# SSD stage of a two-block model: another order of ScalarE's work and of C B, y's gate on VectorE and its square on GpSimd

## The reference, cut to what matters

```python
zxbcdt = h @ w_in
xbc = silu(causal_depthwise_conv(xbc, conv_w, conv_b))      # -> xs, b_in, c_in
a_cs = cumsum(a_dt)
decay = exp(where(causal, a_cs[..., :, None] - a_cs[..., None, :], -inf))
cb = einsum('bclgn,bcsgn->bcgls', c_c, b_c)
y = einsum('bcgjls,bcsgjp->bclgjp', cb * decay, xdt)          # (+ the part of earlier chunks)
y = y + xs * repeat(d_skip, HEAD_DIM)
g = y * silu(z)
g = g * rsqrt(mean(g * g) + EPS)                             # the mean over a group's 256 channels
out = (g * norm_g) @ w_out
```

## Time and profile before

| what | value |
|---|---|
| median of 3 runs | 1209.87 us (1209.8 to 1210.95) |
| the profiled execution's own time | 1210.28 us |
| its span, first to last instruction | 1208.6 us |
| mean granted TensorE clock | 0.973 |
| the stretch from the end of slot 1 to the end of slot 7 on ScalarE | 73.4 to 223.8 us |

### The profile page before, as it was taken

How to read it: one execution, slowest core, us unless ns; L and a number is a source line. 1 busy time by engine, 2 the same in 40 slices (tenths; PEclk the granted TensorE clock), 3 DMA queues, 4 the chain that set the end, 5 groups by cost and what they waited for, 6 DMA issues and landing times.

```text
span 1208.6 us, 23743 instructions
## 1 busy us (share of the span) xinstructions
PE 1148.3 (95%) x8898; PEld 1089.9 (90%) x8898; DVE 754.4 (62%) x1123; ACT 674.9 (56%) x1071; POOL 186.3 (15%) x134
## 2 busy tenths in 40 slices
PE   6999999999999999679988999999999999999998
PEld 5988988899999999556657999999998999999998
DVE  4788778768665554536646666555678678666543
ACT  4788888755554343457735555444554665555332
POOL 0443444317000001022301000000000212000000
PEclk8999999999999999779979999999999999999999
DMA  5554344395555554222203555565544555555553
GB/s 192 179 173 151 130 158 154 113 256 159 180 174 168 182 165 157 88 86 88 80 26 111 186 191 181 183 192 179 170 159 125 172 185 184 188 177 188 192 179 99
DMA packets 53225, 190.32 MB, mean 157 GB/s; under 512 B 5920, under 2 KB 7072, under 8 KB 53168
## 3 DMA queue, kind: packets, MB, share of 16 engines
q1 hardware_dynamic: 51408, 182.95, 47.0%
q0 software_dynamic: 1760, 6.59, 1.8%
HBM read 188.44 MB, written 1.08 MB: 157 GB/s over the span
## 4 chain that ended last, share of the span: by engine, by line
PE 75%; DVE 8%; issue 8%; ACT 5%; POOL 3%; DMA 1%; ACTq 0%; DVEq 0%; POOLq 0%; SPq 0%
PE lin L412 23%; PE lin L414 22%; PE lin L413 22%; DVE w_lo L1207 2%; POOL w_lo L1747 1%; ACT w_hi L826 1%; POOL y L1765 1%; PE lin L641 1%; PE ps L682 1%; PE ps L683 1%; PE lin L639 1%; DVE cv L1286 1%; PE ps L445 1%; DVE rot_a L1509 0%; DVE x_lo L1217 0%
## 5 line engine op out<-in xcount | busy, mean ns | idle before, releaser
L1207 DVE TENSOR_TENSOR w_lo<-w_raw,w_hi 128x1024 fp32r<-128x1024 f32 x303 | 381.3, 1260 | 273.1 <-ACT w_hi L826 273.0
L826 ACT ACTIVATE w_hi<-w_raw 128x1024 fp32r<-128x1024 f32 (+2 forms) x343 | 354.3, 1040 | 244.3 <-PE lin L414 239.9
L412 PE MATMUL lin<-x_hi,w_hi 128*128 128x256 f32 (+1 forms) x1528 | 445.4, 291 | 11.0 <-DVE x_lo L1233 3.7
L414 PE MATMUL lin<-x_hi,w_lo 128*128 128x256 f32 (+1 forms) x1528 | 439.0, 287 | 0.0
L413 PE MATMUL lin<-x_lo,w_hi 128*128 128x256 f32 (+1 forms) x1528 | 438.2, 287 | 0.0
L412 PEld LDWEIGHTS lin<-x_hi,w_hi 128*128 128x128 f32 x1528 | 292.0, 191 | 15.2 <-DVE x_lo L1233 4.1
L413 PEld LDWEIGHTS lin<-x_lo,w_hi 128*128 128x128 f32 x1528 | 291.5, 191 | 1.4 <-issue 1.0
L414 PEld LDWEIGHTS lin<-x_hi,w_lo 128*128 128x128 f32 x1528 | 292.3, 191 | 0.0
L414 PE MATMUL lin<-hid_hi,w_lo 128*128 128x256 f32 (+1 forms) x768 | 218.2, 284 | 0.0
L413 PE MATMUL lin<-hid_lo,w_hi 128*128 128x256 f32 (+1 forms) x768 | 217.9, 284 | 0.0
L412 PE MATMUL lin<-hid_hi,w_hi 128*128 128x256 f32 (+1 forms) x768 | 217.4, 283 | 0.0
(11 more groups left out here) (252 smaller groups left out, 1515.7 us busy)
## 6 DMA issues: line engine op xcount, KB each, us to landing
w_raw<-w SPq DMA_DIRECT2D x343, 512.0 KB, 3.3
acs_bc<-acs_dram POOLq DMA_DIRECT2D x8, 544.0 KB, 4.9
bias_mask<-rpb POOLq DMA_DIRECT2D x4, 512.0 KB, 9.6
h<-h SPq DMA_DIRECT2D x4, 272.0 KB, 3.7
out<-h SPq DMA_DIRECT2D x8, 128.0 KB, 3.4
cst<-const SPq DMA_DIRECT2D x1, 784.0 KB, 8.4
vecs<-vec SPq DMA_DIRECT2D x1, 131.5 KB, 2.1
acs_dram<-y POOLq DMA_DIRECT2D x1, 34.0 KB, 2.5
```

The source lines that it names most:

```text
L412: mm3(o, wh, xh, start=first and i == 0, stop=False)
L414: ins = mm3(o, wl, xh, start=False, stop=last and i == kts - 1)
L826: a(w_hi[pg.slot][:, 0:n], w_raw[pg.slot][:, 0:n], ACT.Copy).then_inc(w_hi_done, pages)
L1207: tt(w_lo[pg.slot][:, 0:n], w_raw[pg.slot][:, 0:n], w_hi[pg.slot][:, 0:n].bitcast(F32), ALU.subtract)\
```

## The change

ScalarE's slot has another order: the decays first, then z's sigmoid, then `hi` and `conv0` of the first pair, `decay_logs(s, 0)` before the first sigmoid of the slot (for s above 0), and `decay_logs(s, 1)` and the second sigmoid ahead of `g_hi`. TensorE does C B before the transposes. VectorE masks C B before the convolution, takes the product y2 = y1 * z_s, and does the first SiLU product before `lo` of page (c+3, 0). GpSimd squares y2, which ScalarE did before.

```diff
 TensorE
                 if has_scan:
+                    cb_products(s + (-1))
                     x_transposes(s + (-1))
-                    cb_products(s + (-1))
 ScalarE
-                if has_lin:
-                    hi((c + 2).page(0))
-                    hi((c + 2).page(1))
                 if has_scan:
                     decay(g, 0)
                     decay(g, 1)
-                if has_stat:
-                    act.wait_ge(y2_done, (gs + 1).value)
-                    a(h_sq[:, 0:2, :], y2[:, :, :], ACT.Square).then_inc(ysq_done, 1)
-                if has_lin:
-                    conv0(s, 0)
-                    hi((c + 3).page(0))
-                    act.wait_ge(clamped, s.times(2, 1).value)
-                    sigmoid(sg[:, 0:2, :], sg_step, s.times(6))
-                if has_scan:
                     kz = g.times(3, K_GRP + 2)
                     act.wait_ge(drained[kz.parity], kz.half + 1)
                     sigmoid(z_sg[:, :, :], zg_step, g.times(3), z_raw[:, :, :])
                 if has_lin:
+                    hi((c + 2).page(0))
+                    conv0(s, 0)
+                    hi((c + 2).page(1))
+                if has_lin:
+                    if s.base:
+                        decay_logs(s, 0)
+                    act.wait_ge(clamped, s.times(2, 1).value)
+                    sigmoid(sg[:, 0:2, :], sg_step, s.times(6))
+                    hi((c + 3).page(0))
                     conv0(s, 1)
                     hi((c + 3).page(1))
                 if not has_lin:
                     hi2(s + (C_SOUT - 6))
-                if has_lin and s.base:
-                    decay_logs(s, 0)
                 if has_stat:
...
                 if has_lin:
+                    if s.base:
+                        decay_logs(s, 1)
                     hi((c + 4).page(0))
+                    act.wait_ge(clamped, s.times(2, 2).value)
+                    sigmoid(sg[:, 2:4, :], sg_step, s.times(6, 3))
                 if has_stat:
...
                 if has_lin:
-                    act.wait_ge(clamped, s.times(2, 2).value)
-                    sigmoid(sg[:, 2:4, :], sg_step, s.times(6, 3))
                     if not s.base:
                         decay_logs(s, 0)
-                    decay_logs(s, 1)
+                        decay_logs(s, 1)
                     hi((c + 4).page(1))
 VectorE
                             (ps6, ps7)[q][:, 0:T], ALU.mult, ALU.add).then_inc(y_read, 1)
+                    dve.wait_ge(y_read, gs.times(2, 2).value)
+                    dve.wait_ge(z_silu_done, (gs + 1).value)
+                    tt(y2[:, :, :], y1[:, :, :], z_s[gs.parity][:, :, :], ALU.mult).then_inc(y2_done, 1)
...
                     lo((c + 2).page(0))
+                    if has_scan:
+                        causal_cb(g)
                     conv(s, 0)
...
                     scaled_tokens(g)
-                    causal_cb(g)
+                    if not has_lin:
+                        causal_cb(g)
...
                 if has_lin:
+                    silu(s, 0, xs_s[s.parity][:, :, :], cv[:, 0:2, :], sg[:, 0:2, :])
                     lo((c + 3).page(0))
-                    silu(s, 0, xs_s[s.parity][:, :, :], cv[:, 0:2, :], sg[:, 0:2, :])
                     conv(s, 1)
 GpSimd
-                    pool.wait_ge(y_read, gs.times(2, 2).value)
-                    pool.wait_ge(z_silu_done, (gs + 1).value)
-                    if gs.base:
-                        pool.wait_ge(y3_done, gs.value)
-                    tt(y2[:, :, :], y1[:, :, :], z_s[gs.parity][:, :, :], ALU.mult).then_inc(y2_done, 1)
+                    pool.wait_ge(y2_done, (gs + 1).value)
+                    tt(h_sq[:, 0:2, :], y2[:, :, :], y2[:, :, :], ALU.mult).then_inc(ysq_done, 1)
                     pool.wait_ge(ysq_done, (gs + 1).value)
                     tt(y_sum[:, :], h_sq[:, 0, :], h_sq[:, 1, :], ALU.add).then_inc(ysum_done, 1)
```

## The result

The changed kernel takes 1234.88 us (median of four, 1233.29 to 1237.52), the kernel before 1210.05 in the same series. The ratio is 1.0206, with a 95% interval of 1.0187 to 1.0225: 2.1% slower. The forecast was 1234 us.

What follows compares the result with a forecast made beforehand. The prediction took TensorE (95% busy) as the bound before and ScalarE's slot, 20.70 + 7.4 = 28.1 us, after. It summed 1210.28 + 18.2 + 6.4 - 0.7 = 1234.2, said 1234 us, range 1223 to 1249.

Steps and rivals of the forecast that it cites:

- What bounds: SSD stage before: slot 25.07 us, TensorE's own work 22.9, ScalarE's work 21.35, so ScalarE has 3.7 slack.
- Taken alone this part gives up to 12.8 us: SSD stage: removing TensorE's mask waits (9.8 us) and their clock loss (3.0) could gain up to 12.8 us.
- the first rival: SSD stage: ScalarE's new wait fits its slack and TensorE regains its waits, 1197.5 us; chance 0.05.
- What is taken away: Each slot: the square leaves ScalarE, whose work becomes 20.70 us; VectorE's product 0.7, GpSimd's square 2.34.
- What is added: ScalarE, seven slots: dd waits 7.4 us for the row transfer, which starts only after GpSimd's lo.
- the second rival: Row transfers: each takes 7.5 us beside page loads, 18 us more, 1252 us; chance 0.12, with parts of it.
- The walk: One slot followed through the engines: TensorE waits some 5 us, but ScalarE sets the slot at 28.1 us.
- H: Start point of the slot timing on ScalarE: the end of hi for page (c+2, 1).
- The sum: Whole kernel: 1210.28 + 18.2 (six slots) + 6.4 (slots 0 and 1) - 0.7 (after slot 7) = 1234.2 us.
- the third rival: TensorE: behind its 5 us waits the clock stays at 1.2 GHz for the whole next chunk, 1240 us; chance 0.11.
- The faster one: Same as the first rival: 1197.5 us if the transfer takes under 1.95 us; chance 0.05.
- The fourth: ScalarE: its work is less through overlap counted twice, slot 26.5 us, 1223 to 1226 us; chance 0.10.

Runs made afterwards that it cites:

- The mask first, alone: Kernel before, with only C B ahead of the transposes on TensorE and its mask ahead of the convolution on VectorE: 1209.45 us, ratio 1.0015.
- y2 alone: Kernel before, with only the y2 product moved to VectorE and its square to GpSimd: 1200.66 us, ratio 0.993.
- dd alone, early: Kernel before, with decay_logs(s, 0) ahead of the first sigmoid and the row transfer of group s+1 started in slot s: 1204.58 us, ratio 0.996.
- dd alone: Kernel before, with only decay_logs(s, 0) moved ahead of the slot's first sigmoid, for s above 0: 1257.41 us, ratio 1.0401.
- rows before lo: Changed kernel, with the row transfer started just ahead of GpSimd's lo of page (c+2, 1) instead of behind it: 1204.31 us, ratio 0.9968.
- rows early: Changed kernel, all orders kept, with the row transfer of group s+1 started already in slot s: 1195.84 us, repeated at 1195.55.

## Why the prediction was right

Point by point:

- **What bounds.** TensorE's waits and ScalarE's slack were read rightly, but not joined. I took the 9.8 us for the mask as a loss that the mask's place makes. The mask first, alone, showed that it doesn't: the same time came back as a wait for the taps. y2 alone, which takes work and a wait off ScalarE, gained instead. "Taken alone this part gives up to 12.8 us" was wrong, and the first rival's 1197.5 us was met only by the whole change with no wait for the rows (1195.6 to 1195.8). TensorE's own work in a slot, 22.9 by my sum, was 22.53 there.
- **What is taken away.** ScalarE's work of 20.70 us held: 28.14 a slot less 7.5 of wait is 20.6. y2's product on VectorE took 0.72 to 0.73 in slots 3 to 8 and 2.81 in slot 2, where 0.7 was taken. GpSimd's square took 1.33 on the mean over slots 2 to 7, a little under the lower bound of 1.4 and far from the 2.34 that I took; it lay in GpSimd's idle time. VectorE paid what I had not put down: its busy time in six slots rose from 117.0 to 132.6 us, 15.7 more: 7.2 for the product, `g_lo` 19.4 instead of 5.5, and `lo` 23.8 instead of 29.9. VectorE still had 36.6 us idle.
- **What is added.** Seven waits were forecast, of 7.4 us, some 50 us in all. There are seven, of 7.3 to 8.1, 53.0 in all. The chain was as told: 0.07 us to GpSimd, 2.34 of `lo`, 5.0 of transfer (4.9 forecast; 5.6 at most, so the second rival didn't come). Its removal takes 39 us off, and its shortening by 31.2 us takes 30.6 off.
- **The walk.** I had `dd` at H + 7.4 and the next conv0 at 26.1. From H at 113.52, `dd` started at 7.57 and the next conv0 at 26.0 (139.52). TensorE's gap was 4.84, forecast 5; the seven gaps, ahead of slots 2 to 7 and of the output projection, are 2.1 to 5.1 us, 3.8 on the mean. One step of the walk was off: TensorE ended the next chunk at H + 24.9 (138.4), not at 22.1, since it ran at half the clock until about 135. That is still 1.1 us ahead of ScalarE.
- **The sum.** 18.2 forecast for six slots, measured 169.2 - 150.4 = 18.8. For slots 0 and 1 6.4 forecast; from the first sigmoid of slot 0 to the end of slot 1 were 34.2 (39.23 to 73.4) and are 40.4 (37.61 to 78.0), 6.2 more. After slot 7 I forecast a gain of 0.7, and there is a loss of 1.6: from the decays of slot 8 to the end of the span 984.8 (223.76 to 1208.6) and 986.5 us (247.22 to 1233.7). TensorE reaches the transposes of slot 8 3.4 us behind ScalarE's decays (250.62 against 247.22), and 0.97 before (224.73 against 223.76); the chunk ahead of them ran at the half clock until about 247.7, behind a wait of 4.27. That is the third rival's mechanism in a place where no ScalarE wait hides it. But it isn't shown to be the cause of the 1.6 us: the same stretch took between 976.7 us (dd alone, early) and 992.0 (dd alone) in the traces of the other kernels, which differ there in slots 8 and 9 at most; from 330 to 430 us behind those decays the clock was 0.98 in the first and 0.85 in the second. The first sigmoid of slot 0 came 1.6 us earlier in this execution; in the traces of all kernels it lies between 37.2 and 39.2. 18.8 + 6.2 + 1.6 - 1.6 = 25.0, and the spans differ by 25.1. That the last two terms cancel is luck; the mechanism and the two large terms are not.
- **The rivals.** The faster one fell at the point that the forecast named: the transfer would have had to land within 1.95 us. The transfer in this place took 4.8 to 5.6. The clock fell behind six of the seven gaps, those of 3.2 to 5.1 us; behind the one of 2.06 us (until 101.75) it stayed at 2.4 GHz, while in the kernel before it had fallen behind one of 1.95. Even so ScalarE came later to conv0 than TensorE, but for one wait of 1.0 us (ahead of 83.59). The fourth, an overlap in ScalarE's work, is out, with 20.6 to 20.7 us. The Trainium skill ("Perfetto Trace Analysis", Identifying the Most-Contended Engine) says to optimize first the engine of highest occupancy. The trace does not bear this out here: TensorE was busiest (95%), and taking away the wait that the profile named on it gained nothing (1.0015), while work taken off ScalarE (56%) gained 0.7%. The bandwidth figures of the Trainium skill, by which I estimated 3.6 us for 544 KB, count only the time in which the DMA engines are busy; from issue to landing the broadcast rows took 5.0, so they could not serve as the price of this wait.

## What to carry to other kernels

When an instruction moves up in an in-order queue, follow each of its waits back to what starts it. Here the transfer started only behind work on the page that the same engine had just made, so no slack could cover it, and the wait could be priced from three rows before a run. Issue such a transfer as soon as its buffer is free, here one slot earlier. And a wait that the profile puts on a product (the mask) need not be the bound: check whether the engine behind it has room in its period before a gain is put down.

## What the runs showed of the hardware that was not expected

GpSimd's time for 544 columns seems to depend on which of the two engines was at work first. In the kernel before the product took 2.34 us (from 100.74), with VectorE's `lo` at work since 99.38 and until 101.86; in slot 8 the same product took 1.36 (at 226.28), where VectorE read PSUM. In the kernel after the square took 1.30, and VectorE paid. Its two `g_lo` instructions, 0.91 us together in the kernel before (at 121.07), took 3.87 where GpSimd's `lo` ran from 107.21 to 110.03 and the square behind it until 111.28:

```profile
107.71 3.87 DVE L1327 SCALAR_TENSOR_TENSOR g_lo<-z_s,vecs,g_hi 128x272 fp32r<-128x272 f32 x2
```

The Trainium skill ("SBUF — State Buffer", SBUF: two separate sides) tells of a pair of ports that VectorE and GpSimd lock for a whole instruction. The 2.34 and the 3.87 us agree with that; that the lock is the cause was not tested by a run.

The transfer of the rows took another time at another place: 5.0 us from issue to landing on the median in the kernel after, 4.4 in rows before lo, 4.0 in dd alone, early, and 5.4 to 5.7 in rows early. No run shows why.
